# Feature-major up and gate products with stationary weight tiles in a fused two-block transformer kernel

## Chip, core and metric

One Trainium2 chip, one core. The metric is the device time of one execution in microseconds; inputs and weights lie in HBM, everything is float32.

## What is computed

Two transformer blocks one after the other on x of 256 tokens by 1024 features. The parts that the change touches are three feed-forward stages:

```python
# block 1, d_ff = 4096
h2 = rms_norm(x, g_mlp)
x = x + square(relu(h2 @ w_ff1)) @ w_ff2
x = x + sigmoid(rms_norm(x, g_ple) @ w_ple_gate) * (p @ w_ple)

# block 2, d_ff_2 = 2816, before and after its attention
x = x + 0.5 * ((silu(h @ w_gate) * (h @ w_up)) @ w_down)    # h = rms_norm(x, ffn_norm)
```

`rms_norm` divides a row by the root of its mean square and multiplies by a gain. Around these stand the projections and attentions of both blocks, which stay as they are.

## The kernel before

**Precision.** Every large product is done with three matmuls in float32r: an operand a is split into a_hi (a rounded to float32r by a copy) and a_lo = a - a_hi, and a_hi w_hi + a_hi w_lo + a_lo w_hi is summed in PSUM. Weights come in 163 units of 128x2048 (SyncE's queue, six raw slots). ScalarE makes w_hi (`hi`, L920), VectorE w_lo (`lo`, L1309). A unit is held until TensorE has counted it in `unit_used`; w_hi has four slots, w_lo lies in the raw slot. A narrow unit has four 128-row tiles of 512 columns, a wide one two of 1024.

**Layout.** Tokens lie on partitions in two row blocks tb of 128. Activations that are multiplied are first transposed: `turn` (L475, matmuls at L481) puts 128x128 blocks into a PSUM bank, `split` makes hi (ScalarE, L926) and lo (VectorE, L1316). `product` and `products` (L450, L458, matmuls at L467) take the transposed activation block (128x128) as the stationary operand and 512 columns of weights as the moving one; in the profile's names the moving operand stands first (`bank<-w_hi,hA_hi`).

**The three stages.** "ff" has 8 steps of 512 features, "f1" and "f2" 11 steps of 256 gate and 256 up features. A step i computes the up (and gate) products of step i into two banks `up(tb)` (`ff_up`, L665: two units, each over two row blocks), transposes the activations of step i - 1 in the middle (`ff_turn`, L659) and then multiplies those by the down weights into the four accumulator banks. The first step of a stage (`ff_up0`, L654) starts with row block 0 while the norm's operand of block 1 is still being made. ScalarE applies relu or silu with the row scale 1/rms out of the bank (L1076, L1149), VectorE multiplies with the bank's content (L1522, L1595) into act_f and frees the bank with `up_out`. In a gated stage's tail (L752 to L763) the last up products go by row block (`narrow_block`), with the transposes in between.

**Order.** Each engine's program is written out by hand; the engines meet only at semaphores. TensorE's order decides; the others run ahead as far as slots allow. GpSimd computes 1/rms (L1812, L1813, L1882) and loads gains.

Of the kernel before, what the change touches and what calls it, by code (L numbers as in the profile page):

```python
# [28 lines left out]
P = 128  # L29
D, TB, SEQ = 1024, 2, 256  # L30
# [63 lines left out]
def work_batches():  # L94
# [17 lines left out]
    order += [("ff", i, tb) for i in range(DFF // HALF) for tb in range(TB)]  # L112
    order += [("ple", tb, h) for tb in range(TB) for h in range(2)]
    order += [("ffn1", tb, h) for tb in range(TB) for h in range(2)]
    order += [("f1", i, tb) for i in range(FF2 // SUB) for tb in range(TB)]
# [9 lines left out]
    order += [("f2", i, tb) for i in range(FF2 // SUB) for tb in range(TB)]  # L125
# [3 lines left out]
def score_maps():  # L129
# [23 lines left out]
    [x for x in WB if x[0] in ("p", "ya", "yr", "m", "ff", "f1", "f2", "cq", "ckv", "cat", *NORMS)])}  # L153
# [6 lines left out]
def two_blocks(nc, x_d, p_d, g_mix, w_in, lam_q1, lam_k1, lam_q2, lam_k2, g_diff, g_ret, w_bd, w_br, w_out,  # L160
# [39 lines left out]
    hA = [sb(f"hA_{s}", [P, KT, SEQ], f32r) for s in ("hi", "lo")]  # L200
# [12 lines left out]
    def lay(start, *parts):  # L213
# [14 lines left out]
    qk_tm = lay(named["yr"], ("qk_tm0", [P, TB, HALF]), ("qk_tm1", [P, TB, HALF]))  # L228
    lam_v, lam_w = lay(named["ga"], ("lam_v", [P, 4, DHD]), ("lam_w", [P, 2, DHD]))
# [6 lines left out]
    fT0, fT1, act_r, act_f, pl_s, sg, pT0, pT1, p_sb, gain_mid = lay(  # L236
        arena, ("fT_hi", [P, 4, SEQ], f32r), ("fT_lo", [P, 4, SEQ], f32r), ("act_r", [P, TB, HALF]),
        ("act_f", [P, TB, HALF]), ("pl_s", [P, TB, D]), ("sg", [P, TB, D]),
        ("pT_hi", [P, 2, SEQ], f32r), ("pT_lo", [P, 2, SEQ], f32r), ("p_sb", [P, TB, 256]), ("gain_mid", [P, D]))
# [23 lines left out]
    up = lambda tb: bank[4 + tb]  # L263
    score = lambda name: bank[4 + SM[name] % 2]
    work = lambda name: bank[6 + WB[name] % 2]
# [10 lines left out]
    nhalf_ready, act_warm = sem("nhalf_ready"), sem("act_warm")  # L276
# [21 lines left out]
    up_done, act_ready, up_out = sem("up_done"), sem("act_ready"), sem("up_out")  # L298
# [124 lines left out]
    def rows_of(name):  # L423
# [6 lines left out]
        if kind in ("ff", "f1", "f2"):  # L430
            tb, k0, n, pair = name[2], 0 if kind == "ff" else 2 * (name[1] % 2), 4 if kind == "ff" else 2, fT
        elif kind == "cq":
            tb, k0, n, pair = name[1], 0, 3, cT
        else:
            tb, k0, n, pair = name[1], 4 * name[2], 4, hB if kind in ("ya", "m", "ple") else hA
# [13 lines left out]
    def _(pe):  # L449
# [204 lines left out]
        def ff_up0(u0, norm):  # L654

            narrow_block(up(0)[:, :], norm, u0, 0, HALF, lambda: src_turn(norm, 1)).then_inc(up_done, 1)
            narrow_block(up(1)[:, :], norm, u0, 1, HALF)

        def ff_turn(name, i, done, cols, di=0, blocks=range(TB)):  # L659

            for tb in blocks:
                pe.wait_ge(up_out, done - 1 + tb + 2 * di)
                turn((name, i, tb), [act_f[:, tb, j * P:(j + 1) * P] for j in range(cols // P)], di)

        def ff_up(u, name, i, steps, cols, du=0, di=0):  # L665

            for j in range(2):
                for tb in range(TB):
                    if j == 0:
                        pe.wait_ge(up_out, 2 * steps - 1 + tb + 2 * di)  # L670
                    mm = products([up(tb)[:, :]], hA, 4 * j, 4, tb, u + j, HALF, j == 0, j == 1, du)
                    if j and tb == 0:
                        mm.then_inc(up_done, 1)
                mm.then_inc(unit_used, 1)
                if j == 0:
                    ff_turn(name, i - 1, 2 * steps, cols, di)
# [3 lines left out]
        ff_up0(u, "mlp")  # L680
# [3 lines left out]
        def relu_step(i, r=0, start=False):  # L684
            v = U0["ff"] + 2 + 4 * (i - 1)
            ff_up(v, "ff", i, i, HALF, 12 * r, 3 * r)
            for j in range(2):
                for tb in range(TB):
                    if j == 0:
                        turned(("ff", i - 1, tb), 3 * r)  # L690
# [10 lines left out]
        ff_turn("ff", last, 2 * (last + 1), HALF)  # L701
# [1262 lines left out]
```

## Time and profile before

| | |
|---|---|
| runs | 1019.32 to 1019.88 us, median 1019.78 (3 runs) |
| the profiled execution | 1019.78 us, its span 1018.0 us |
| TensorE busy, of the span | 992.1 us (97%) in 4730 matmuls |
| VectorE busy | 578.5 us (57%) |
| ScalarE busy | 489.1 us (48%) |
| GpSimd busy | 72.3 us (7%) |
| DMA | 179.27 MB, mean 176 GB/s |

A matmul's record is longer than the distance to the next one, since matmuls are pipelined: distances between starts tell the price. PEld is the load of the stationary operand, which has a record of its own.

### The profile page before, as it was taken

The page shows a single profiled execution, that of the slowest core. Times are in us where ns is not written, and L with a number is a line of the kernel's source. Part 1 is how long each engine was busy: PE and PEld are TensorE (multiplying, and loading weights), DVE is VectorE, ACT ScalarE, POOL GpSimd, SP SyncE. Part 2 cuts the span into 40 slices and gives each one's busy share as a digit, 9 for nine tenths or more (in the row PEclk, how much of TensorE's full clock was granted, in tenths as well). Part 3 has the DMA queues.
Part 4 walks back from the last instruction along what each step waited for, and adds up shares of the span by engine and source line. Part 5 has one row for each costly group of instructions (what it writes and reads, how often), then busy time and mean ns, then how long its engine had stood idle before and what let it go on. Part 6 is the DMA issues. An engine that isn't in the chain of part 4 may idle for free.

```text
span 1018.0 us, 12693 instructions
## 1 busy us (share of the span) xinstructions
PE 992.1 (97%) x4730; PEld 821.4 (81%) x4730; DVE 578.5 (57%) x700; ACT 489.1 (48%) x613; POOL 72.3 (7%) x95
## 2 busy tenths in 40 slices
PE   6999999999999999999999999999999999999997
PEld 4888788888888888888778888888877888888885
DVE  4655555487675555555775455447555675555443
ACT  5545455744355344444563434335557454444431
POOL 3100000040020000000320000001111000000000
PEclk9999999999999999999999999999999999999999
DMA  9755545444465555454555555545552165556531
GB/s 322 249 193 167 163 134 187 144 154 186 165 238 207 192 186 185 171 200 166 203 174 202 177 195 183 188 149 176 175 204 65 44 208 184 196 177 205 168 122 42
DMA packets 99744, 179.27 MB, mean 176 GB/s; under 512 B 5856, under 2 KB 53872, under 8 KB 99696
## 3 DMA queue, kind: packets, MB, share of 16 engines
q1 hardware_dynamic: 97424, 171.99, 48.7%
q0 software_dynamic: 1984, 6.30, 2.0%
q8 instruction: 31, 0.51, 0.2%
q10 hardware_dynamic: 288, 0.33, 0.1%
q14 instruction: 17, 0.14, 0.0%
HBM read 177.55 MB, written 1.05 MB: 175 GB/s over the span
## 4 chain that ended last, share of the span: by engine, by line
PE 93%; DVE 3%; ACT 1%; issue 1%; POOL 1%; DMA 1%; DVEq 0%; POOLq 0%; ACTq 0%
PE bank L467 84%; PE bank L481 5%; PE bank L517 1%; PE bank L516 1%; DVE w_lo L1309 1%; DMA masks<-const_masks 1%; PE bank L528 0%; PE bank L530 0%; PE bank L529 0%; POOL rs L1813 0%; POOL ms L1812 0%; DVE x L1561 0%; PE bank L794 0%; PE bank L793 0%; DVE sg L1560 0%
## 5 line engine op out<-in xcount | busy, mean ns | idle before, releaser
L1309 DVE TENSOR_TENSOR w_lo<-raw,w_hi 128x2048 fp32r<-128x2048 f32 (+2 forms) x163 | 370.9, 2280 | 221.0 <-ACT w_hi L920 220.9
L920 ACT ACTIVATE w_hi<-raw 128x2048 fp32r<-128x2048 f32 (+2 forms) x163 | 308.1, 1891 | 159.9 <-PE bank L467 157.2
L467 PE MATMUL bank<-w_hi,hA_hi 128*128 128x512 f32 (+1 forms) x880 | 343.0, 396 | 5.1 <-DVE w_lo L1399 3.0
L467 PE MATMUL bank<-w_hi,hA_lo 128*128 128x512 f32 (+1 forms) x880 | 337.1, 389 | 0.0
L467 PE MATMUL bank<-w_lo,hA_hi 128*128 128x512 f32 (+1 forms) x880 | 336.7, 389 | 0.0
L467 PEld LDWEIGHTS bank<-w_hi,hA_hi 128*128 128x128 f32 x880 | 165.4, 188 | 38.7 <-issue 4.7
L467 PEld LDWEIGHTS bank<-w_hi,hA_lo 128*128 128x128 f32 x880 | 165.6, 188 | 34.7
L467 PEld LDWEIGHTS bank<-w_lo,hA_hi 128*128 128x128 f32 x880 | 165.9, 188 | 32.4
L467 PE MATMUL bank<-w_hi,fT_hi 128*128 128x512 f32 x304 | 93.8, 390 | 0.0
L467 PE MATMUL bank<-w_lo,fT_hi 128*128 128x512 f32 x304 | 93.6, 389 | 0.0
L467 PE MATMUL bank<-w_hi,fT_lo 128*128 128x512 f32 x304 | 93.6, 389 | 0.0
L926 ACT ACTIVATE fT_hi<-bank 128x256 fp32r<-128x256 f32 (+1 forms) x60 | 23.4, 439 | 117.4 <-PE bank L481 117.4
L467 PEld LDWEIGHTS bank<-w_lo,fT_hi 128*128 128x128 f32 x304 | 57.1, 188 | 11.9
L467 PEld LDWEIGHTS bank<-w_hi,fT_lo 128*128 128x128 f32 x304 | 57.1, 188 | 11.9
L467 PEld LDWEIGHTS bank<-w_hi,fT_hi 128*128 128x128 f32 x304 | 56.8, 188 | 11.6
L1316 DVE TENSOR_TENSOR fT_lo<-bank,fT_hi 128x256 fp32r<-128x256 f32 (+1 forms) x60 | 27.1, 491 | 62.6 <-ACT fT_hi L926 62.5
L1812 POOL TENSOR_SCALAR ms<-ss 128x1 f32<-128x1 f32 x16 | 7.8, 486 | 628.1 <-ACT junk L944 628.0
L1149 ACT ACTIVATE act_r<-bank,rs 128x256 f32<-128x256 f32 x44 | 20.9, 475 | 57.5 <-PE bank L467 55.0
L1595 DVE SCALAR_TENSOR_TENSOR act_f<-bank,rs,act_r 128x256 f32<-128x256 f32 x44 | 21.2, 481 | 21.6 <-ACT act_r L1149 21.6
L973 ACT ACTIVATE L<-L,mn 128x128 f32<-128x128 f32 x64 | 28.4, 458 | 10.1 <-DVE mn L1356 10.0
L944 ACT ACTIVATE junk<-x 128x1024 bf16<-128x1024 f32 x16 | 16.9, 1055 | 33.9 <-DVE x L1342 21.7
L467 PE MATMUL bank<-w_hi,hB_hi 128*128 128x512 f32 x96 | 30.2, 396 | 0.0
(236 smaller groups left out, 759.3 us busy)
## 6 DMA issues: line engine op xcount, KB each, us to landing
raw<-in_w_in SPq DMA_DIRECT2D x76, 512.0 KB, 4.5
raw<-in_w_ff SPq DMA_DIRECT2D x64, 512.0 KB, 3.9
raw<-in_ffn_w_gate SPq DMA_DIRECT2D x44, 512.0 KB, 3.6
raw<-in_ffn_w_up SPq DMA_DIRECT2D x44, 512.0 KB, 4.5
raw<-in_ffn_w_down SPq DMA_DIRECT2D x44, 512.0 KB, 4.0
raw<-in_w_out SPq DMA_DIRECT2D x16, 512.0 KB, 3.8
raw<-in_w_branch_diff SPq DMA_DIRECT2D x8, 512.0 KB, 3.7
raw<-in_w_branch_ret SPq DMA_DIRECT2D x8, 512.0 KB, 3.7
```

The costliest lines, as they stand in the source:

```text
L467: mm = pe.matmul(o, a, w, start=first and t == 0 and m < len(outs), stop=last and t == n - 1 and m >= len(todo) - len(outs))
L481: mm = pe.transpose(work(name)[0:cols, col:col + rows], blk, ident)
L516: pe.matmul(b[:, 0:P], q[:, h, 0:P], k[:, h, 0:P], start=True, stop=True)
L517: pe.matmul(b[:, P:384], q[:, h, P:SEQ], k[:, h, :], start=True, stop=True).then_inc(score_done, 1)
L920: act.activation(w_hi[u % HI_SLOTS][:, 0:w], raw[u % RAW_SLOTS][:, 0:w], ACT.Copy).then_inc(hi_ready, 1)
L926: act.activation(dst, b, ACT.Copy).then_inc(split_hi, 1)
L944: act.activation(junk[:, :], x[:, tb, :], ACT.Square, accum_out=ss[:, n:n + 1]).then_inc(square_sum, 1)
L973: e = act.activation(L[:, m % 4, c], L[:, m % 4, c], ACT.Exp, bias=mn[:, m, tb:tb + 1], scale=-1.0, accum_out=sm[:, m, tb:tb + 1])
L1149: act.activation(act_r[:, tb, 0:SUB], up(tb)[:, 0:SUB], ACT.Silu, scale=inv_rms(norm, tb))\
L1309: vec.tensor_tensor(w_lo[u % RAW_SLOTS][:, 0:w], raw[u % RAW_SLOTS][:, 0:w], w_hi[u % HI_SLOTS][:, 0:w].bitcast(f32), ALU.subtract).then_i ...
L1316: vec.tensor_tensor(dst, b, hi.bitcast(f32), ALU.subtract).then_inc(work_out[WB[name] % 2], 1)
L1595: vec.scalar_tensor_tensor(out=act_f[:, tb, 0:SUB], in0=up(tb)[:, SUB:2 * SUB], scalar=rs[:, n:n + 1], in1=act_r[:, tb, 0:SUB], op0=ALU.mu ...
```

## The change

The up and gate products change their operands' roles. For each 128-column weight tile f (four per step, `TILES`) and each k-tile there are two matmuls with the weight tile stationary: w_hi against h_hi and h_lo of all 256 tokens in one matmul of 512 columns (`both`; hA_hi and hA_lo now lie in one tensor hA2), and w_lo against h_hi, 256 columns (`one`). A bank `tall(f)` (banks 4 to 7) then holds 128 features by 256 tokens twice: the low half and a high half that belongs to h_lo. ScalarE copies one half out, VectorE adds the other (`tile_sum`), and the activation comes out with features on partitions, as the down products want it; `ff_turn` is gone. `f_split` makes hi and lo from SBUF.

A row scale is now a scale along columns. In "ff" it is left out of the activation and applied in `x_add` (relu(hr)^2 = r^2 relu(h)^2). In the gated stages the gate is multiplied by rsb, 1/rms spread over all partitions: GpSimd makes diagonal matrices (`rstd_rows`, `diag`), TensorE multiplies them by ones into bank 0 ahead of the last quarter of the first step, VectorE copies that out. The up half's scale goes with the 0.5 into `x_add` (`rsh`).

The first step (`first_tiles`) goes by row block and unit: 64 pairs of matmuls of 256 and 128 columns. The last step of a gated stage goes tile by tile like the others, with no work between. The transposes of "mlp", "ffn1" and "ffn2" go to the accumulator banks, as banks 6 and 7 are in use.

```diff
+        def tall_product(f, u, t, kt, cols, first, last):
+            at = t * HALF + f * P
+            hi, lo = w_hi[u % HI_SLOTS][:, at:at + P], w_lo[u % RAW_SLOTS][:, at:at + P]
+            both = halves(f)[:, :, cols], hi, hA2[:, :, kt, cols]
+            one = halves(f)[:, 0, cols], lo, hA2[:, 0, kt, cols]
+            for m, operands in enumerate((one, both) if last else (both, one)):
+                mm = pe.matmul(*operands, start=first and m == 0, stop=last and m == 1, skip_group_check=True)
+            return mm
+        def first_tiles(name, norm, order, beside=None):
...
+            for tb in range(TB):
+                cols = slice(tb * P, (tb + 1) * P)
+                for j in range(2):
+                    turned((norm, tb, j))
+                    if tb and j and beside:
+                        beside()
+                    pe.wait_ge(lo_ready, u + j + 1)
+                    for n, f in enumerate(order):
+                        for t in range(4):
+                            mm = tall_product(f, u + j, t, 4 * j + t, cols, (tb, j, t) == (0, 0, 0),
+                                              (tb, j, t) == (1, 1, 3))
...
+        def tiles(name, u, i, order, du=0, ds=0):
+            s = STEP0[name] + i
             for j in range(2):
-                for tb in range(TB):
+                pe.wait_ge(lo_ready, u + j + 1 + du)
+                for n, f in enumerate(order):
                     if j == 0:
-                        pe.wait_ge(up_out, 2 * steps - 1 + tb + 2 * di)
-                    mm = products([up(tb)[:, :]], hA, 4 * j, 4, tb, u + j, HALF, j == 0, j == 1, du)
-                    if j and tb == 0:
+                        pe.wait_ge(up_out, TILES * (s - 1) + n + 1 + TILES * ds)
+                    for t in range(4):
+                        mm = tall_product(f, u + j, t, 4 * j + t, slice(0, SEQ), (j, t) == (0, 0), (j, t) == (1, 3))
+                    if j and n < TILES - 1:
                         mm.then_inc(up_done, 1)
                 mm.then_inc(unit_used, 1)
-                if j == 0:
-                    ff_turn(name, i - 1, 2 * steps, cols, di)
...
+            def rstd_rows():
+                pe.wait_ge(ones_ready, 1)
+                pe.wait_ge(diag_ready, TB * (GATED[name] + 1))
+                for tb in range(TB):
+                    mm = pe.matmul(bank[0][:, tb * P:(tb + 1) * P], ones[:, :], diag[:, tb, :], start=True, stop=True)
+                mm.then_inc(rsb_done, 1)
+
+            first_tiles(name, norm, PAIRED, rstd_rows)
...
             v, i = u + 2 + 3 * (n - 2), n - 1
-            pe.wait_ge(up_out, 2 * (base + i))
-            narrow_block(up(0)[:, :], None, v, 0, HALF, lambda: ff_turn(name, i - 1, 2 * (base + i), SUB))\
-                .then_inc(up_done, 1)
-            narrow_block(up(1)[:, :], None, v, 1, HALF, lambda: ff_turn(name, i, 2 * (base + n), SUB, blocks=(0,)))
+            tiles(name, v, i, PAIRED)
             down(v + 2, i - 1, 0)
-            ff_turn(name, i, 2 * (base + n), SUB, blocks=(1,))
             down(v + 3, i, 0, last=True).then_inc(acc_done, 1)
...
+            # ScalarE, gated stages
+            def silu(i, k, r=0):
+                last_unit = u + 1 + (3 * i - 1 if i else 0)
+                for n, f in ((2 * k, k), (2 * k + 1, 2 + k)):
+                    half_copy(name, i, n, f, act_s[:, f, :], last_unit, 4 * r, 12 * r)
+                act.wait_ge(gate_in, PAIR0[name] + 2 * i + k + 1 + 8 * r)
+                act.activation(act_r[:, k, :], act_s[:, k, :], ACT.Silu).then_inc(gate_out, 1)
...
+            # VectorE, gated stages
+            def multiply(i, k, r=0):
+                tile_sum(name, i, 2 * k, k, act_s[:, k, :], 4 * r)
+                vec.tensor_tensor(act_s[:, k, :], act_s[:, k, :], rsb[:, :], ALU.mult).then_inc(gate_in, 1)
+                tile_sum(name, i, 2 * k + 1, 2 + k, act_s[:, 2 + k, :], 4 * r)
+                vec.wait_ge(gate_out, PAIR0[name] + 2 * i + k + 1 + 8 * r)
+                vec.tensor_tensor(act_f[:, k, :], act_r[:, k, :], act_s[:, 2 + k, :], ALU.mult).then_inc(act_ready, 1)
...
-                x_add(name, 0, 0.5, norm_out)
+                x_add(name, 0, half_rs[0], norm_out)
                 split_rows(norm_out, 0)
-                x_add(name, 1, 0.5, norm_out)
+                lo(v + 5)
+                x_add(name, 1, half_rs[1], norm_out)
```

## Rows read from the trace of the kernel before

**Rows 1.** The page: busy us, share and instructions of each engine; granted clock by slice.
```profile
PE 992.1 (97%) x4730; PEld 821.4 (81%) x4730; DVE 578.5 (57%) x700; ACT 489.1 (48%) x613; POOL 72.3 (7%) x95
...
PEclk9999999999999999999999999999999999999999
```

**Rows 2.** The page, chain that ended last: share of the span by engine.
```profile
PE 93%; DVE 3%; ACT 1%; issue 1%; POOL 1%; DMA 1%; DVEq 0%; POOLq 0%; ACTq 0%
```

**Rows 3.** Windows, a ReLU and a gated step: us, busy (instructions) of PE, PEld, DVE, ACT, POOL, clock.
```profile
379.16:401.84 22.68, 22.68 (x106) 18.88 (x105) 11.75 (x8) 9.91 (x8) 0.00 (x0) 1.00 0.51 185
526.90:543.70 16.80, 16.80 (x78) 13.90 (x77) 8.61 (x8) 7.12 (x8) 0.00 (x0) 1.00 0.56 189
```

**Rows 4.** The chain in order of time (start, us, what): the transposes of either kind of step.
```profile
401.82 0.87 PE bank L481 x8
...
543.28 0.44 PE bank L481 x4
```

**Rows 5.** Timeline of PE (start, us, shape) at 512 and 288 columns; the chain at 384.
```profile
400.06 0.39 PE L467 MATMUL bank<-w_hi,hA_lo 128*128 128x512 f32 x1
...
401.42 0.40 PE L467 MATMUL bank<-w_hi,hA_lo 128*128 128x512 f32 x1
...
708.13 0.29 PE L467 MATMUL bank<-w_hi,hA_hi 128*128 128x288 f32 x1
...
714.39 0.29 PE L467 MATMUL bank<-w_hi,hA_lo 128*128 128x288 f32 x1
...
751.97 3.15 PE bank L467 x18
```

**Rows 6.** Timeline of PE: float32 products of 64 columns, two instructions each.
```profile
766.03 0.39 PE L792 MATMUL bank<-mv,aT 128*128 128x64 f32 x2
766.25 0.39 PE L793 MATMUL bank<-mv,aT 128*128 128x64 f32 x2
```

**Rows 7.** The first gated stage's tail: two pieces of the chain, then PE's timeline.
```profile
675.42 5.48 PE bank L467 x24
681.12 5.47 PE bank L467 x24
...
693.11 0.66 PE L481 MATMUL bank<-masks,src 128*128 128x128 f32 x4 [0.39 <-DVE src L1335]
```

**Rows 8.** PE's timeline around the first gated stage's first two steps.
```profile
511.75 0.66 PE L481 MATMUL bank<-masks,src 128*128 128x128 f32 x4 [1.28 <-DVE src L1335]
512.16 0.47 PE L467 MATMUL bank<-w_hi,hA_hi 128*128 128x512 f32 x1
512.47 0.39 PE L467 MATMUL bank<-w_lo,hA_hi 128*128 128x512 f32 x1
...
522.94 0.39 PE L467 MATMUL bank<-w_hi,hA_lo 128*128 128x512 f32 x1
523.45 0.50 PE L467 MATMUL bank<-w_hi,hA_hi 128*128 128x512 f32 x1
```

**Rows 9.** GpSimd there, from the timeline; then a line's instructions, ns min/median/max.
```profile
517.48 2.47 POOL L1813 TENSOR_TENSOR rs<-ms,nhalf 128x1 f32<-128x1 f32 x1
520.03 2.27 POOL L1882 TENSOR_TENSOR rs<-rs 128x1 f32<-128x1 f32 x1
...
L1823 POOL TENSOR_SCALAR bias<-masks x8: 511/512/2652, 25.3 to 153.1; 128x384 f32<-128x384 f32 x8
```

**Rows 10.** Groups by line and form: busy us, mean ns of one, idle before.
```profile
L1309 DVE TENSOR_TENSOR w_lo<-raw,w_hi 128x2048 fp32r<-128x2048 f32 x157 | 362.2, 2311 | 219.1 <-ACT w_hi L920 219.0
...
L1595 DVE SCALAR_TENSOR_TENSOR act_f<-bank,rs,act_r 128x256 f32<-128x256 f32 x44 | 21.2, 481 | 21.6 <-ACT act_r L1149 21.6
...
L926 ACT ACTIVATE fT_hi<-bank 128x256 fp32r<-128x256 f32 x44 | 14.7, 382 | 86.5 <-PE bank L481 86.5
```

**Rows 11.** Timeline at the second gated stage's start: GpSimd's second scale, VectorE's w_lo.
```profile
828.44 0.56 POOL L1813 TENSOR_TENSOR rs<-ms,nhalf 128x1 f32<-128x1 f32 x1
...
829.88 4.48 DVE L1309 TENSOR_TENSOR w_lo<-raw,w_hi 128x2048 fp32r<-128x2048 f32 x2
```

## What the change does to the time, told before it was run

> **What bounds the kernel now.** I read the page from its totals downwards. TensorE is busy for 97% of the span, and the slices give it the full granted clock throughout, so no part of the sum rests on the clock [rows 1]. VectorE and ScalarE are near half [rows 1], so they matter only where someone waits for them. The chain that ended last is 93% TensorE: 84% of the span are the products of L467, 5% the transposes of L481 [rows 2]. A change here is worth what it takes from or adds to TensorE's instruction stream, plus waits at the joints of stages. The stages show no slack: a whole ReLU step lasts 22.68 us and a whole gated step 16.80 us, with TensorE busy in all of it and VectorE and ScalarE in about half [rows 3]. The chain in order of time splits such a step into 96 (72) products and 0.87 (0.44) us for 8 (4) transposes [rows 4].
>
> A busy time says little about a pipelined product: its record lasts 389 ns, but the next begins 0.227 us later. All prices below are distances between starts.
>
> **The price of a product by width.** 512 columns: from 400.06 to 401.42 are six distances, 0.227 us each [rows 5]. 384 columns: 3.15 us for 18, 0.175 [rows 5]. 288 columns: 708.13 to 714.39 is 47 distances, 0.133 [rows 5]. The line through 512 and 288 has 0.419 ns a column; 256 columns lie just beyond its end, at 0.120. There is also a floor that does not come from the columns: float32 products with only 64 columns, each with a stationary load of its own, still come 0.11 apart (two start at 766.03, the next two at 766.25) [rows 6]. So a product with 128 columns costs 0.110, not the 0.067 of the line.
>
> Here a rule bears on the case. The load floor of 0.11 is what the rows show [rows 6]. The Trainium skill (TensorE: Matmul & The Clock Gate, "LDWEIGHTS") gives a load as the stationary columns over 1.2, 107 ns for 128; by that rule, the trace agrees. The same page ("Packing small matmuls", on what overlaps) has loads overlap with products only where row groups differ, which speaks against a change that makes 16 more loads a step; by it 27 steps would take 27 x 16 x 0.107 = 46 us more (an estimate from that page). The 288-column products, 0.133 apart with a load each, leave no room for that [rows 5].
>
> **Removed: the transposes of the activations.** The ReLU stage has 8 steps with 8 each, 8 x 0.87 = 7.0 us. Each gated stage has ten steps' worth of 4 (0.44) and two pairs in its tail: 675.42 plus 5.48 is 680.90 and the next piece starts at 681.12, 0.22 a pair [rows 7]. That is 2 x (10 x 0.44 + 2 x 0.22) = 9.7. Together 152 transposes (64 and 88) and -16.6 us. The figure includes the slow first product behind each block (0.31 instead of 0.227, as from 512.16 to 512.47) [rows 8]. All of it is on the path.
>
> **Changed: the up and gate products.** Before, a step takes 8 k-tiles x 2 row blocks x 3 products of 512 columns: 48 x 0.227 = 10.90 us. After, 8 k-tiles x 4 weight tiles x (one of 512 and one of 256 columns): the columns are the same 24,576, the instructions are 64. Cost 32 x (0.227 + 0.120) = 11.10, so +0.21 a step. There are 8 + 11 + 11 = 30 steps, of which 27 are whole: +5.6 us. The bounds: with 256 columns at the load floor of 0.110 the step costs 10.78 and the 27 give -3.1; at the nearest measured fp32r width, 0.133, they give +16.8. I take 0.120, since three widths lie near one line and the nearest is only 32 columns away.
>
> **The first step of each stage** is cut by row block, since the second block's operand arrives later. It has 64 pairs of 256 and 128 columns: 64 x (0.120 + 0.110) = 14.7 against 10.90, +3.8 a stage, +11.5 for three. This is where the change pays most: the 128-column product does half the work of a 256-column one for nearly the same price. Bounds for it: 0.067, if the load hides entirely (-2.8 a stage), and 0.22, the two instructions of 0.11 that a float32 product takes [rows 6] (+7 a stage). No fp32r product under 288 columns is in the trace; I take 0.110 as the load floor is nearest to what binds.
>
> **The joints.** Before the first gated stage TensorE stands 1.28 us for src before the transposes of 511.75 [rows 8]; the first quarter's extra 0.9 us hides in it: -0.9. Then its three remaining quarters of 3.7 us begin at 512.16: two end at 519.5. There the new stationary-ones products wait for diag, which GpSimd makes behind the second rs. GpSimd's small operations stretch to VectorE's end of w_lo (2.47 us from 517.48; 2.27 from 520.03, just behind the start of the next w_lo) [rows 9]. In the new order VectorE waits for rsb after L1309's pair, so the second of these should take about 0.2, at 520.2. The two diag of 128 columns, a third of the 384 that take 0.51 [rows 9], take 0.3 each; with the hops diag is there at 521.0: +1.5. The ones products are 2 x 2 float32 instructions of 0.11 and a slow first one: 0.5 in each gated stage, +1.0. The wait of 0.28 before 523.45 goes (the new step's banks are four, freed in turn): -0.3 [rows 8]. In the second gated stage the second rs is there at 829.0 and TensorE comes to it eight microseconds later, so that diag is covered even if it waits until 834.4 for the w_lo of 829.88 [rows 11].
>
> At the end of a gated stage the last step's activations are no longer computed beside the second row block. After the last tile there are a ScalarE copy 0.38, a VectorE sum 0.48, a product 0.48, ScalarE's split 0.38 and VectorE's 0.48, with hops near 2.5 us [rows 10]; TensorE has 12 products (2.73 us) before it asks. Just covered: 0, and up to +1 in each if a hop is longer. Moving w_lo of the next unit behind the first x_add takes away the 0.39 wait at 693.11 [rows 7]: -0.4, though it delays the second x_add by some 0.6.
>
> **What hides the vector work.** A gated step gets four ScalarE copies, four VectorE sums, two products by rsb and the same two products of gate and up; the conversions L920 and L1309 stay, and x_add does the same operation with its scale read from a tile. VectorE: 3 x 2.29 + 10 x 0.45 = 11.4 of 16.6 us; in a ReLU step 4 x 2.29 + 12 x 0.45 = 14.6 of 22 [rows 10]. The deadline is the bank: tile n of the next step needs up_out n. The first tile is ready 9.6 us before TensorE returns to it, and so is each next one. Queued in front of its sum stands one w_lo, which starts 7.5 us into the step and ends at 9.8; the four sums are out by 13.0 and the first is wanted at 16.6. Cost nothing; were this cover gone, every late microsecond would count 27 times.
>
> **Sum.** -16.6 + 5.6 + 11.5 - 0.9 + 1.5 + 1.0 - 0.3 - 0.4 = +1.4 us on a span of 1018.0. The profiled execution took 1019.78, 1.8 more than its span, and is the median itself: 1021.2. The transposes saved are given back in halves: to the fixed part of more, shorter products and to the three cut first steps.
>
> **Rivals.**
> *The short product is cheaper.* If the 256-column product runs at the load floor, every step wins: 27 x 32 x 0.010 = 8.6, and 3 x 64 x 0.010 = 1.9 in the first steps: 1010.7. For it: eight transposes with a load each take 0.87, the slow product behind them included, so not over 0.109 each [rows 4]. Against it: three fp32r widths all carry about 13 ns [rows 5]. The Trainium skill (TensorE: Matmul & The Clock Gate, "Back-to-back issue gap") has columns/2.4 + 2.5 ns for a single product, 109 ns for 256; it also makes 512 cost 216, where the trace has 227. Chance 0.15, 1008 to 1015.
> *The short product is dearer*, the rival on the slower side. One mechanism: fp32r widths under the measured ones do not follow the line, since the load becomes what is waited for. At 0.133 for both short widths: 27 x 32 x 0.013 + 3 x 64 x (0.013 + 0.023) = 18, 1039; with only the 128-column ones at 0.22, 3 x 64 x 0.11 = 21, 1042. It decides from 0.121 upwards for the 256-column product, so a nanosecond counts 1 us. For it: nothing that narrow was run, and loads and columns nearly tie (0.110 and 0.107). Against: the floor and the line both lie under 0.121. Chance 0.25, 1028 to 1042.
> *Waits replace transposes.* The hand-over between three engines in tails and joints, or ScalarE's hand-back of gate_in and gate_out, comes late, by 5 to 14 us in all: 1026 to 1035. Against it is the slack of 3.6 us in every step. Chance 0.1.
>
> **How the numbers follow.** Forecast 0.5, 1018 to 1025. About 0.2%, 2 us, is what a measurement can tell from no change: faster means under 1017.7, slower over 1021.8. The forecast lies close to that upper line and gives 0.05, 0.25 and 0.2 to faster, same and slower; the others 0.15 faster and 0.35 slower. Faster 0.2, same 0.25, slower 0.55. The range 1010 to 1034 holds the forecast, nearly all of the cheap case, the waits and the nearer end of the dear one: 0.8.
>
> **What would show it.** In the new profile: no transposes of act_f; distances of 0.227 and 0.120 in turn in a whole step, which should last 22.0 (ReLU) and 16.6 us (gated); 14.7 us for a first step's 128 products; TensorE standing about 1.5 us ahead of the first ones products; no TensorE wait for VectorE sums inside steps. A distance of 0.110 or 0.133 makes the prediction wrong by itself.

## The result and the profile after

| | before | after |
|---|---|---|
| median of the runs | 1019.83 us (1019.32 to 1020.01) | 1029.3 us (1027.99 to 1031.62) |
| the profiled execution, its span | 1019.78, 1018.0 us | 1028.2, 1026.4 us |
| ratio, 95% interval | | 1.0096 (1.008 to 1.0112) |
| predicted | | 1021.2 (1010 to 1034) |

The changed kernel is slower by about 9.5 us, 1%. The forecast gave 0.55 to slower, and slower it is, but by more: its likeliest case, 1018 to 1025, did not come. The time lies inside the range, 8 us above the point, where two of the rivals had put theirs ("the short product is dearer", 1028 to 1042, and "waits replace transposes", 1026 to 1035). That the range held is in part luck, since neither rival's mechanism accounts for most of it.

The page of the changed kernel, busy time by engine and then the chain's shares:

```profile
PE 998.8 (97%) x5258; PEld 847.4 (83%) x5258; DVE 641.3 (62%) x898; ACT 516.3 (50%) x733; POOL 71.7 (7%) x104
...
PE 93%; DVE 3%; ACT 1%; issue 1%; POOL 1%; DMA 1%; DVEq 0%; POOLq 0%; ACTq 0%
```

Against [rows 1] and [rows 2] the shape is the same: TensorE is 97% busy and 93% of the chain, now with 528 more matmuls. By line, the pages give the chain of before 84% of products (L467) and 5% of transposes (L481), and that of the changed kernel 53% (L482) and 33% (L676, the changed ones) of products and 3% of transposes (L496). VectorE got 63 us of work and ScalarE 27, and neither became the bound. So the lost time has to be looked for in TensorE's own stream and at the joints.

The windows of a ReLU step, a gated step and, further down, two stretches behind the second block's attention (us, then busy and instructions of PE, PEld, DVE, ACT, POOL, then the granted clock):

```profile
332.68:354.83 22.15, 22.15 (x113) 18.82 (x113) 13.55 (x16) 10.08 (x12) 0.00 (x0) 1.00 0.55 190
...
543.25:559.97 16.72, 16.72 (x90) 14.32 (x89) 10.67 (x14) 8.28 (x11) 0.00 (x0) 1.00 0.57 188
...
812.00:816.00 4.00, 3.41 (x22) 3.13 (x22) 1.07 (x3) 0.50 (x2) 0.00 (x0) 0.82 0.01 4
816.00:818.00 2.00, 2.00 (x8) 1.63 (x7) 1.55 (x3) 0.85 (x2) 0.00 (x0) 0.51 0.00 0
```

A whole step did become shorter than before, 22.15 against 22.68 and 16.72 against 16.80 [rows 3], but not as short as forecast (22.0 and 16.6). In the last two stretches the granted clock is 0.82 and 0.51: it falls to its lower level of 1.2 GHz, half of the full one, which the forecast had nowhere.

Where the 8.4 us of span came in is read by putting the same places of the two chains side by side. First the chain of before (start, us, what): the last transposes ahead of "ff", the end of "ff", a copy behind "f1", two groups of transposes of the second block, the end of "f2".

```profile
289.79 0.87 PE bank L481 x8
...
494.37 0.56 issue
...
736.98 0.70 DVE mqT L1729
...
810.58 1.09 PE bank L481 x8
...
821.24 0.88 PE bank L481 x8
...
1010.65 1.30 DVE x L1640 x2
```

The same places in the chain of the changed kernel:

```profile
290.81 0.87 PE bank L496 x8
...
494.68 0.56 issue
...
740.94 0.70 DVE mqT L1803
...
814.51 1.97 PE bank L496 x8
...
826.76 0.87 PE bank L496 x8
...
1018.98 1.42 DVE x L1714 x2
```

The lag is 1.02, 0.31, 3.96, 3.93, 5.52 and 8.33 us. Its steps, with what the forecast's own terms give for each stage:

| stretch | forecast | measured |
|---|---|---|
| up to "ff" (first load of constants and what follows) | 0 | +1.0 |
| "ff": 3.8 + 7 x 0.21 - 7.0 | -1.7 | -0.7 |
| "f1": 4.6 for the joint and first step, + 10 x 0.21 - 4.8 - 0.4 | +1.5 | +3.65 |
| second block's attention up to 810.58 | 0 | 0.0 |
| 810.58 to 821.24, where the clock fell | 0 | +1.6 |
| "f2": 4.3 + 10 x 0.21 - 4.8 | +1.6 | +2.8 |
| sum | +1.4 | +8.35 |

### The profile page after: what moved, and what is told of

The parts are those of the page before. It is cut to its first block, busy times and chain, and to the rows that moved or that the text cites. A ratio compares the mean times of both kernels' runs of the same rounds, so it can differ in the third digit from the quotient of the medians.

```text
span 1026.4 us, 14193 instructions
## 1 busy us (share of the span) xinstructions
PE 998.8 (97%) x5258; PEld 847.4 (83%) x5258; DVE 641.3 (62%) x898; ACT 516.3 (50%) x733; POOL 71.7 (7%) x104
## 4 chain that ended last, share of the span: by engine, by line
PE 93%; DVE 3%; ACT 1%; issue 1%; POOL 1%; DMA 1%; DVEq 0%; POOLq 0%; ACTq 0%
PE bank L482 53%; PE bank L676 33%; PE bank L496 3%; PE bank L532 1%; PE bank L531 1%; DVE w_lo L1363 1%; DMA masks<-const_masks 1%; PE bank L543 0%; ACT junk L989 0%; DVE hA L1370 0%; PE bank L545 0%; PE bank L544 0%; POOL rs L1887 0%; DVE x L1396 0%; DVE sg L1629 0%
## 5 line engine op out<-in xcount | busy, mean ns | idle before, releaser
L676 PE MATMUL bank<-hA,w_hi 128*128 128x512 f32 (+1 forms) x1056 | 345.8, 385 | 1.3 <-issue 1.3
L676 PE MATMUL bank<-hA,w_lo 128*128 128x256 f32 (+1 forms) x1056 | 266.2, 271 | 0.0
L482 PE MATMUL bank<-w_hi,hA 128*128 128x512 f32 (+1 forms) x800 | 247.8, 392 | 4.1 <-DVE w_lo L1453 3.0
L676 PEld LDWEIGHTS bank<-hA,w_hi 128*128 128x128 f32 x1056 | 192.2, 188 | 32.4 <-issue 1.7
L676 PEld LDWEIGHTS bank<-hA,w_lo 128*128 128x128 f32 x1056 | 198.8, 189 | 9.5
L482 PEld LDWEIGHTS bank<-w_hi,hA 128*128 128x128 f32 x800 | 150.3, 189 | 34.8 <-issue 4.6
L482 PE MATMUL bank<-w_lo,hA 128*128 128x512 f32 (+1 forms) x400 | 150.2, 388 | 0.0
L482 PE MATMUL bank<-w_hi,fT_hi 128*128 128x512 f32 x304 | 93.9, 390 | 0.0
L482 PE MATMUL bank<-w_lo,fT_hi 128*128 128x512 f32 x304 | 93.6, 389 | 0.0
L482 PE MATMUL bank<-w_hi,fT_lo 128*128 128x512 f32 x304 | 93.6, 389 | 0.0
L482 PEld LDWEIGHTS bank<-w_lo,hA 128*128 128x128 f32 x400 | 75.9, 190 | 14.7
L1125 ACT ACTIVATE act_s<-bank 128x256 f32<-128x256 f32 x120 | 42.9, 375 | 69.1 <-PE bank L676 69.1
L482 PEld LDWEIGHTS bank<-w_lo,fT_hi 128*128 128x128 f32 x304 | 57.1, 188 | 12.0
L482 PEld LDWEIGHTS bank<-w_hi,fT_lo 128*128 128x128 f32 x304 | 57.1, 188 | 11.9
L482 PEld LDWEIGHTS bank<-w_hi,fT_hi 128*128 128x128 f32 x304 | 57.0, 188 | 11.0
L1577 DVE TENSOR_TENSOR act_s<-bank,act_s 128x256 f32<-128x256 f32 x120 | 50.2, 419 | 23.9 <-ACT act_s L1125 23.8
```

What stands on the lines that cost most here:

```text
L482: mm = pe.matmul(o, a, w, start=first and t == 0 and m < len(outs), stop=last and t == n - 1 and m >= len(todo) - len(outs))
L676: mm = pe.matmul(*operands, start=first and m == 0, stop=last and m == 1, skip_group_check=True)
L1125: act.activation(dst, halves(f)[:, 1, :], ACT.Copy).then_inc(half_out, 1)
L1577: vec.tensor_tensor(dst, halves(f)[:, 0, :], dst, ALU.add).then_inc(up_out, 1)
```

## Experiments

The first theory was that the excess in whole steps is a property of the product pair, 0.352 us where the sum has 0.347, that the first steps cost what was forecast, and that what is above 1028 in a run is the clock. The experiments change first the pair, then the first step, then the joint, and last the widths. The runs of before beside them had medians of 1019.85 (the first four kernels), 1020.33 (after_again to e8_all512) and 1019.98 us.

**The moving operand in one piece.** The `both` product reads h_hi and h_lo from two places 2048 elements apart. Here they lie side by side for each k-tile.

```diff
-            hA2 = sb("hA", [P, 2, KT, SEQ], f32r)
+            hA2 = sb("hA", [P, KT, 2, SEQ], f32r)
...
```

> The changed kernel with one thing different: h_hi and h_lo lie side by side per k-tile, so the 512-column product of a whole step reads one contiguous stretch instead of two of 256. In the changed kernel a pair costs 0.352 us, 0.234 from the 512-column product to the 256-column one and 0.118 back. Theory A, the two-stretch operand costs 7 ns: the 0.234 falls to 0.227, a whole step from 11.27 to 11.05, and the 27 steps give 5 to 6 us. Theory B, the 7 ns come from the order (a 512-column product whose stationary operand is loaded behind a short one): the distances stay, the time stays within 1 us of the changed kernel's at the same granted clock.

Measured: 1029.96 us (1028.35 to 1033.41), ratio to before 1.0089 (1.0069 to 1.0109), no different from the changed kernel. The up products of one step in its chain:

```profile
332.57 11.27 PE bank L683 x64
```

11.27 us again: how the operand lies plays no part. The profiled execution was the longest of these, 1033.41 us, with a mean clock of 0.991, and shows where this one lost its time. Its windows (columns as above):

```profile
508.00:510.00 2.00, 0.81 (x4) 0.84 (x5) 2.00 (x4) 2.00 (x4) 1.27 (x3) 0.67 0.93 314
510.00:514.00 4.00, 4.00 (x21) 4.00 (x20) 3.69 (x6) 2.26 (x2) 0.00 (x0) 0.50 0.28 100
...
524.00:526.00 2.00, 0.24 (x3) 0.12 (x2) 0.00 (x0) 1.75 (x1) 1.92 (x6) 0.94 0.27 26
526.00:532.00 6.00, 6.00 (x28) 6.00 (x29) 1.70 (x4) 1.91 (x4) 0.79 (x3) 0.50 0.70 254
```

Twice TensorE stood for longer, 2.90 us until 509.19 and 1.76 us until 525.98, and each time the clock was at 0.50 in the stretch behind it. Six microseconds at half the clock are three microseconds of work lost. Both stands belong to the first gated stage's start; the second is the wait for diag that the change added.

**All w_hi products of a tile, then all w_lo products.** Same products, another order.

```diff
-                    for t in range(4):
-                        mm = tall_product(f, u + j, t, 4 * j + t, slice(0, SEQ), (j, t) == (0, 0), (j, t) == (1, 3))
+                    for m in ((1, 0) if j else (0, 1)):        # 0: both, 1: one
+                        for t in range(4):
+                            mm = pe.matmul(*tall_operands(f, u + j, t, 4 * j + t, slice(0, SEQ))[m], ...)
...
```

> The changed kernel with another order inside a tile: four 512-column products (w_hi) one after the other, then four of 256 columns (w_lo), instead of alternating; operands as before. Theory B (a 512-column product behind a 256-column one starts late): only one in four still stands behind a short one, three in four fall to 0.227, a whole step from 11.27 to about 11.1, 4 us in all. Theory A (two-stretch operand): 512-column products stay at 0.234 wherever they stand, no gain. For the 256-column products in a row both say 0.118 to 0.120; at 0.133 the load would be what binds.

Measured: 1028.34 us (1026.95 to 1031.83), ratio 1.0073 (1.0057 to 1.009). A step in the chain:

```profile
332.51 11.20 PE bank L717 x64
```

and on TensorE's timeline (start, us, what):

```profile
400.02 1.09 PE L717 MATMUL bank<-hA,w_hi 128*128 128x512 f32 x4
400.95 0.63 PE L717 MATMUL bank<-hA,w_lo 128*128 128x256 f32 x4
401.42 1.09 PE L717 MATMUL bank<-hA,w_hi 128*128 128x512 f32 x4
```

11.20 instead of 11.27: the order gives back 0.07 a step, 1.9 us in 27, less than half of what was expected (the fastest run is 1.0 us under the changed kernel's fastest). Eight products take 1.40 us, 0.350 a pair. Part of the excess belongs to the change of width from one product to the next; the rest stayed.

**A cheaper first step.** The w_hi products stay cut by row block; the w_lo products are done once, for both row blocks, when the second one's operand is there: 96 products instead of 128.

```diff
-                        for t in range(4):
-                            mm = tall_product(f, u + j, t, 4 * j + t, cols, ...)
+                        if tb:
+                            for t in range(4):
+                                pe.matmul(*tall_operands(f, u + j, t, 4 * j + t, slice(0, SEQ))[1], ...)
+                        for t in range(4):
+                            mm = pe.matmul(*tall_operands(f, u + j, t, 4 * j + t, cols)[0], ...)
...
```

> The changed kernel with the first step of each stage done differently: w_hi products by row block as before (256 columns), but w_lo once for both row blocks (256 columns instead of twice 128), so 96 products instead of 128. Theory, the load sets the price of every short product: 96 x 0.120 = 11.5 instead of 14.7 us, 3.2 us less in the first and third stage. In the second most of it is lost, since TensorE then only waits longer for the diagonal matrices (1.8 us in the changed kernel, up to 4.5 here): 6.5 to 7.5 us in all. Rival, the columns set the price (128 columns cost half of 256): the columns are the same and nothing is gained.

Measured: 1024.22 us (1021.56 to 1024.91), ratio 1.0036 (1.0027 to 1.0046). The fastest execution (mean clock 0.998) is 6.4 us under the changed kernel's fastest, where 6.5 to 7.5 was expected; the others, at 0.994 to 0.997, are up to 3.4 us longer. The timeline shows the price of 256 columns among themselves:

```profile
298.81 0.64 PE L701 MATMUL bank<-hA,w_hi 128*128 128x256 f32 x4
299.29 0.64 PE L698 MATMUL bank<-hA,w_lo 128*128 128x256 f32 x4
```

From 298.81 to 299.29 are four products, 0.120 each: the value the line gave. The 0.120 was right for products of this width alone.

**The removed transposes, priced by doubling them.** The kernel before, with the transposes of the activations done twice.

```diff
-                turn((name, i, tb), [act_f[:, tb, j * P:(j + 1) * P] for j in range(cols // P)], di)
+                turn((name, i, tb), [act_f[:, tb, j * P:(j + 1) * P] for j in range(cols // P)], di, 2)
...
```

> The kernel before with each transpose of the activations done twice into the same bank: 152 more. If they cost on the path what the prediction's sum takes for their removal, 8 take 0.87 and the added ones have no slow product of their own: 152 x 0.109 = 16.6 less some 20 x 0.08 and 8 x 0.08 for that product, so 14 to 16.6 us more than before. Rival, they partly fill gaps in which TensorE would wait for the activations anyway: under 10 us more, and a wait of TensorE would shrink in the trace.

Measured: 1037.27 us (1036.76 to 1038.73), ratio 1.017 (1.0153 to 1.0187), +17.4 us. A group in its chain:

```profile
382.25 1.75 PE bank L482 x16
```

Twice 0.87 [rows 4]: the second eight cost what the first eight do. The 17.4 lies a little over the 14 to 16.6 that was expected, and well over the rival's limit of 10: no wait was hidden behind the transposes. What this prices is adding them. That removing them gave the same is seen in a whole step: 22.15 us are 11.27 of up products and 10.88 of down products, with nothing between. So the miss lies in what was added.

**The changed kernel again**, beside the next ones.

> The changed kernel itself, for the spread of its times against the granted clock. In the two kernels derived from it the granted clock fell to 0.50 behind TensorE's stands of 1.5 to 2.5 us at the first gated stage's start (506 to 510 and 524 to 526) and cost some 2.5 us each time; the profiled execution of the changed kernel had none there and took 1028.2. Theory: its executions fall into levels, about 1028 without such a fall and 2 to 3 us higher for each, with a lower mean clock; the kernel before has the first of the two stands too, but seldom a fall. Rival: the spread has nothing to do with the clock, times and clock are not ordered alike.

Measured: 1028.87 us (1028.05 to 1031.30), ratio 1.0092 (1.0077 to 1.0108); mean clock 0.997 in the shortest, 0.995 in the longest. Time and clock are ordered alike, but the levels that were expected (1028 without a fall of the clock, 2 to 3 us more for each) are not there: in the profiled execution, 1028.40 us, the clock was at 0.50 from 510 to 512 and at 0.72 to 514, behind a stand of 2.55 us.

**The scale's rows behind the first step.** The ones products follow the whole first step instead of standing ahead of its last quarter; VectorE's and ScalarE's copies and sums of step 0 go ahead of rsb.

```diff
-            first_tiles(name, norm, PAIRED, rstd_rows)
+            first_tiles(name, norm, PAIRED)
+            rstd_rows()
...
```

> The changed kernel with the products by ones put behind the first step instead of ahead of its last quarter, and the first step's copies and sums ahead of the multiplication by rsb on ScalarE and VectorE. TensorE then reaches diag after it is there: the stand of 1.8 us goes, up to 1 us of it may come back as a wait for rsb or for the first sums at step 1: 1 to 2 us less than the changed kernel in an undisturbed execution. If the stand also brings the clock down, the median gains 1 to 2 us more. Rival: something else is late then by as much, and the first whole step starts at the same time.

Measured: 1026.56 us (1025.1 to 1028.76), ratio 1.0065 (1.0051 to 1.0079): 3.0 us less in the fastest run and 2.3 in the median. The chain at the first gated stage's start:

```profile
506.02 2.54 issue
508.56 5.44 PE bank L676 x32
...
514.89 11.09 PE bank L676 x96
525.98 0.44 PE bank L775 x4
526.42 11.18 PE bank L676 x64
```

The stand ahead of the ones products is gone. What that is worth shows best beside the trace of after_again, which has the same stand ahead of the stage (2.55 us) and the same fall of the clock behind it: there the down products of step 1 start at 539.57, here at 537.61, 1.96 us earlier, and the whole execution is 1.84 us shorter. That is the stand (1.76 there) and little else; what the fastest runs have beyond it, 1.1 us, isn't explained.

Another stand remains, 2.54 us ahead of the stage's first product, which the chain puts down to "issue". The traces settle what it is. The product waits for the low part of hA, as in the kernel before (0.90 us until 507.01, put down to `hA_lo`): VectorE writes it in two operations, 1.28 us together, from 507.77 here and from 506.88 in the changed kernel, and the stage's first product starts behind the first of them, at 508.56 and 507.67. VectorE is late by one earlier operation, the product `sg`, which ran beside GpSimd's product of two gains. First this run, then the changed kernel:

```profile
495.00 2.38 POOL L1968 TENSOR_TENSOR gain<-gain,gain_mid 128x1024 f32<-128x1024 f32 x1 [4.76 <-DMA gain<-in_ffn_norm]
495.58 2.35 DVE L1633 TENSOR_TENSOR sg<-sg,pl_s 128x512 f32<-128x512 f32 x1 [5.13 <-ACT sg L1172]
...
494.11 2.39 POOL L1959 TENSOR_TENSOR gain<-gain,gain_mid 128x1024 f32<-128x1024 f32 x1 [3.50 <-DMA gain<-in_ffn_norm]
495.96 1.08 DVE L1629 TENSOR_TENSOR sg<-sg,pl_s 128x512 f32<-128x512 f32 x1 [5.13 <-ACT sg L1171]
```

The next `sg`, with GpSimd idle, takes 0.69. In all twelve traces of this document the stand is 0.1 to 0.2 us longer than this `sg`: 0.90 to 1.28 where it took 0.78 to 1.08 (before, e4_turn_twice, the changed kernel, e3_first, e6_best), and 2.22 to 2.90 where it took 2.03 to 2.71 (the other seven). How far the two operations overlap hangs on when the load of the gain lands, and that differs between two executions of the same kernel: GpSimd waited 3.50 us for it in the changed kernel's first trace and 4.78 in after_again's.

**All of it together.** The order of e2_grouped, the first step of e3_first, and the ones products behind the second weight tile of step 1, with VectorE's and ScalarE's splits of step 0 ahead of the next unit's conversion.

```diff
                 for n, f in enumerate(order):
+                    if beside and (j, n) == (0, 2):
+                        beside()
...
+            for m, f in enumerate((0, 2, 1, 3)):
+                tile_sum(name, 0, m, f, act_s[:, f, :])
+            lo(u + 4)
...
-                lo(v + 3, 12 * r)
+                if i > 1:
+                    lo(v + 3, 12 * r)
                 for k in range(2):
                     f_split(name, i - 1, k, 2 * ((i - 1) % 2) + k, 8 * r)
+                if i == 1:
+                    lo(v + 3, 12 * r)
...
```

> The parts together: w_lo once per stage start (96 instead of 128 products), four long and four short products in a row in whole steps, and the products by ones only after the second weight tile of step 1, with the activations of step 0 reordered on ScalarE and VectorE. From 1028.0 undisturbed: 27 x 0.07 = 1.9 for the order, 3.2 each in the first and third stage, 3.2 in the second as the wait for diag no longer stands in the way, and 1.5 of the stand: 1028.0 - 13.0 = 1015, some 0.4% under the kernel before. Rival: the second stage's start is held by the chain from rms through GpSimd whatever the order, so that its 4.7 us stay: 1019.5, no difference to the kernel before.

Measured: **1016.79 us** (1016.49 to 1018.04), ratio 0.9968 (0.9956 to 0.998), faster than both kernels, by 0.3% than the one before. 1015 was expected. The chain:

```profile
519.35 2.80 PE bank L724 x16
...
522.59 8.41 PE bank L724 x48
```

and the window of the joint (columns as above):

```profile
506.00:520.00 14.00, 12.11 (x97) 11.54 (x96) 11.24 (x14) 9.14 (x14) 6.46 (x10) 1.00 0.37 120
```

TensorE still stands for 1.9 of these 14 us, in two pieces of 0.50 and 1.40, behind one of 1.25 just before, and the clock stays whole. e3_first had nearly the same three (1.03, 0.50, 1.40), and there it fell behind them, to 0.50 from 510 to 512; so it isn't shown that the shape of the stands is what kept it. The three savings in the fastest runs come near: 1028.05 - 1.9 (e2) - 6.4 (e3) - 3.0 (e5) = 1016.7 beside 1016.49, partly by luck, since the 3.0 is 1.1 more than the traces explain. The runs lie closer together than the changed kernel's, 1.6 us instead of 3.3; those of before beside them span 1.7.

**Every product 512 columns.** The w_lo product multiplies h_lo too (this adds the term of the two low parts to the result): new roles of the operands at the old width.

```diff
-            one = halves(f)[:, 0, cols], lo, hA2[:, 0, kt, cols]
+            one = halves(f)[:, :, cols], lo, hA2[:, :, kt, cols]
```

> The changed kernel with w_lo against both halves of h, so that the products of whole steps all have 512 columns (it adds the low-low term; the first steps' w_lo products have 256). 512-column products cost 0.234 in the changed kernel, 0.230 in a row of four, 0.227 in the kernel before. Theory, mixing widths costs: among equals they come 0.227 apart, 64 x 0.227 = 14.5 us a step. Rival, the new roles cost (weights stationary, h moving): 0.230 to 0.234, 14.7 to 15.0 us a step. The time is 27 x 3.3 to 3.7 higher, near 1120.

Measured: 1117.57 us. A step's 64 products:

```profile
336.32 14.51 PE bank L676 x64
```

0.2267 each, what 512 columns cost in the old roles [rows 5]. A stationary weight tile instead of a stationary activation block costs nothing in itself.

**The second product 288 and 384 columns wide**, in the layout of e1_contiguous (either adds a part of the low-low term). L says that a load has to fit behind the product before it, M that a change of width costs something by itself.

```diff
-            return both, (halves(f)[:, 0, cols], lo, hA2[:, kt, 0, cols])
+            if cols == slice(0, SEQ):
+                return both, (tall(f)[:, 0:288], lo, hA2[:, kt].rearrange("p s t -> p (s t)")[:, 0:288])
+            return both, (halves(f)[:, 0, cols], lo, hA2[:, kt, 0, cols])
```

> The contiguous form of the changed kernel, with the w_lo product of whole steps widened from 256 to 288 columns (32 columns of the low-low term are added). At equal widths the new roles cost 0.2267 us for 512 columns, and 256-column products in a row 0.120, so that a pair should cost 0.347; it costs 0.352 alternating and 0.350 in fours. Theory L, the next load hardly fits behind 256 columns (two loads in a first step's pair take 0.230, 0.115 each, against 0.120): with 288 columns it fits, and the pair costs what the line says, 0.227 + 0.133 = 0.360, 11.52 us a step. Theory M, unequal widths in turn cost 5 ns whatever they are: 0.365, 11.68 us a step.

> As the run with 288 columns, with 384. Theory L: 0.227 + 0.175 = 0.402, 12.85 to 12.9 us a step. Theory M: 0.407, 13.0 us a step.

Measured: 1038.42 and 1082.53 us. The up products of a step at 288:

```profile
332.86 11.62 PE bank L685 x64
```

and at 384:

```profile
335.22 13.07 PE bank L685 x64
```

Together with the others, against the sum of the two widths' own prices (0.227, 0.175, 0.133, 0.120):

| second product | pair | sum of its parts | excess |
|---|---|---|---|
| 256, in turn | 0.352 | 0.347 | 5 ns |
| 256, in fours | 0.350 | 0.347 | 3 ns |
| 288, in turn | 0.363 | 0.360 | 3 ns |
| 384, in turn | 0.408 | 0.402 | 6 ns |
| 512 | 0.453 | 0.453 | 0 |

At 384 columns a load of 0.11 fits easily and the excess is the largest, so L has fallen. What holds is M's bare statement: pairs of unequal width cost 3 to 6 ns more than their parts, pairs of equal width nothing. What makes it so was not found: M expected the same excess at every width, and it isn't quite. Two things go together in all these pairs and were not separated, the width of the moving operand and the part of the bank that is written. The two widened forms and the one with 512 columns were run once each; their rows are of steps at full clock.

## Why the prediction was off, step by step

**The whole steps' products: the term that was mis-sized.** The forecast took 0.227 + 0.120 for a pair, 11.10 a step and +5.6 us in all. TensorE's timeline of the changed kernel:

```profile
400.03 0.40 PE L676 MATMUL bank<-hA,w_hi 128*128 128x512 f32 x1
400.26 0.28 PE L676 MATMUL bank<-hA,w_lo 128*128 128x256 f32 x1
400.38 0.40 PE L676 MATMUL bank<-hA,w_hi 128*128 128x512 f32 x1
...
401.79 0.40 PE L676 MATMUL bank<-hA,w_hi 128*128 128x512 f32 x1
```

From 400.03 to 401.79 are five pairs, 0.352 each; a step's 32 take 11.27. The 27 whole steps so cost 27 x 0.37 = +10.0 instead of +5.6: 4.4 us of the miss of 7. Both single prices were right (e3_first: 0.120; e8_all512: 0.227), only their sum was not the pair's. The prediction said that a nanosecond on this product counts 1 us, and gave the forecast's own range, 1018 to 1025, room for under four of them: five came. No row of before has a pair of unequal widths; the working did not name this gap.

The Trainium skill (TensorE: Matmul & The Clock Gate, "Back-to-back issue gap") gives a single product as columns over 2.4 and 2.5 ns more, 109 ns for 256. The runs show 120, so the rival that leaned towards it had the wrong sign. The same page's rule that a load overlaps only with products of other row groups (in its part "Packing small matmuls") does not hold here either: 256 columns with a load each, all rows used, came 0.120 apart.

**The first steps: right.** The chain of the changed kernel (start, us, what), "ff" and then "f1":

```profile
294.45 3.65 PE bank L676 x32
...
298.98 11.09 PE bank L676 x96
...
522.17 0.68 PE bank L775 x4
522.85 14.96 PE bank L676 x96
```

3.65 + 11.09 = 14.74 for the 128 products of "ff"; 14.7 was forecast. A pair of 256 and 128 columns takes 0.230, the 0.120 + 0.110 of the forecast. Only the pair is measured: no run has 128-column float32r products among themselves, so that the 0.110 holds alone is not shown. This was the place where the change paid most, and e3_first got more than half of it back by doing 32 products fewer in each stage.

**The transposes: right.** -16.6 was forecast, e4_turn_twice has 17.4 (15.6 to 19.1 by its interval), and the chain has none in the steps.

**The first gated stage's joint: right in kind, 0.9 too small.** Forecast +4.6 up to the start of step 1, measured +5.5. GpSimd and TensorE there, from the timeline:

```profile
518.10 2.47 POOL L1887 TENSOR_TENSOR rs<-ms,nhalf 128x1 f32<-128x1 f32 x1
...
520.65 0.19 POOL L1967 TENSOR_TENSOR rs<-rs 128x1 f32<-128x1 f32 x1
...
520.82 1.20 POOL L1903 TENSOR_SCALAR diag<-masks,rs 128x128 f32<-128x128 f32 x2
...
522.17 0.68 PE L775 MATMUL bank<-diag,ones 128*128 128x128 f32 x4 [1.80 <-POOL diag L1903]
```

The mechanism is the one told: the first rs stretched to 2.47, the second done in 0.19 while VectorE waits, then the diagonals, and TensorE standing. But each diagonal takes 0.60, not 0.3: I had scaled 0.51 for 384 columns [rows 9] by the columns, and that row multiplies by a constant where this one reads a scale for every partition (that this makes the difference is not shown). The 0.9 is made of three parts: the stand was 1.80 instead of 1.5, the ones products took 0.68 instead of 0.5, and the stage's first product came 0.35 late, as the stand ahead of it grew from 0.90 to 1.28 with VectorE's `sg` (under e5_late_rows). In the second gated stage there is no such stand, as forecast; its ones products cost 0.50 and the stage's start +4.3.

**The tails: right.** No wait where I had allowed 0 to +1; ahead of the stage's last piece the 0.39 of [rows 7] has gone.

**What hides the vector work: right.** In no step does TensorE wait for a sum or a copy.

**The clock: left out.** I read the whole clock on the page of before [rows 1] and let no part of the sum rest on it. That was true of the trace of before, but the page can't show it: its slices are 25 us long, and the page of the changed kernel has the same row of nines. In that kernel's profiled execution the clock fell once, between 814 and 818 us (windows above). The eight transposes that took 1.09 in before, with the clock at 1.00 and the same stand of 0.59 ahead of them, took 1.97, and the stretch to 826.76 lost 1.6 us. No edit of this change is at that place, and in e2_grouped it fell there too, so this 1.6 is a matter of the execution.

At the first gated stage's start it fell in most traces of the changed forms. Directly behind the stand ahead of the stage it fell to about 0.50 in each of the seven traces where that stand was 2.22 to 2.90 us, and not in before, e4_turn_twice, the changed kernel and e6_best (0.90 to 1.28; e3_first fell only behind its next two stands). Behind the wait for diag, 1.76 to 1.91 us in seven traces, it fell in four (e1_contiguous, e2_grouped, e3_first, e10_one384) and not in the changed kernel, after_again and e9_one288, nor in e8_all512, where the wait was 1.46. So the forecast priced a stand of TensorE at its own length, and in some executions it cost more: in e1_contiguous the stretch behind the second stand lost three more microseconds.

The changed kernel's runs, ordered, are 1027.99 (mean clock 0.999), 1028.2 (0.997), 1030.4 (0.995) and 1031.62 (0.993). That the clock makes the whole spread is argued, not shown: the mean holds the kernel's last microseconds at 0.50 too, and e6_best has 0.997 without any other fall. Taking 1.6 and 1.8 us for the falls off the two profiled executions, 1028.2 and 1028.40, leaves 1026.6 for both, an estimate, and none of the eight executions was that short. Before spans 0.7 us in the four executions of the result and 2.8 in the thirteen beside the first experiments.

**The first microseconds.** +1.0 us up to "ff" is the load of the constants (5.90 us after, 5.26 before) and 0.35 in the projection ahead of "ff", where the edit does nothing. Neither is of the change's terms. But the first part is not noise of the changed kernel: the load took 5.87 to 6.13 us in all ten traces of the changed forms, 5.76 in e4_turn_twice and 5.26 in the one trace of before. Why was not tried.

Sum of the miss on the span, 8.4 - 1.4 = 7.0: pairs 4.4, joint 0.9, clock 1.6, start 1.0, which is 7.9; the 0.9 too much is 0.1 in "ff" and 0.4 in each gated stage, where nothing was found for it. The median lies another 1.1 us above the profiled execution. Of the rivals, "dearer" came nearest: its mechanism (a load that isn't hidden) was wrong, but its warning that one nanosecond decides was right. "Waits replace transposes" held in one joint only.

**Open.** Why products of unequal width cost 3 to 6 ns more in turn. Whether the clock falls behind a stand of 1.8 us: it did in some traces and not in others. And what the changed kernel gains if GpSimd's product of the gains is moved away from VectorE's `sg`: it was not tried.

## What to carry to other kernels

Price a stream of products as the stream that it will be: the price of each width by itself was right to the nanosecond here, and the pair was 5 ns dearer, which 864 pairs made 4.4 us. When a wide product is cut for the sake of an early start, count the narrow products at the 0.11 us or so that even 128 columns cost, and do them once for all pieces. A stand of TensorE at a joint can cost more than its length, when the clock falls behind it: move small waiting products behind work that is ready, rather than ahead of it (1.8 to 2.0 us here between two traces with the same clock). And where a wait is put down to "issue", follow the engine that makes the operand back through its own operations: here one on VectorE had stretched from 0.8 to 2.4 us beside one of GpSimd, and TensorE stood as much longer.

## What the runs showed of the hardware

- float32r products one after the other: 0.227 us at 512 columns, 0.175 at 384, 0.133 at 288, 0.120 at 256; with 128 columns in turn with 256, 0.230 a pair.
- Unequal widths in turn: 3 to 6 ns a pair above that; equal widths: none.
- A moving operand in two pieces 2048 elements apart cost the same as one in a single piece.
- Directly behind stands of TensorE of 2.22 to 2.90 us the granted clock fell to about 0.50 in seven traces of seven; behind stands of 1.76 to 1.91 us in four of seven. In e1_contiguous it stayed there for 4 and 6 us.
- Stands of 1.25, 0.50 and 1.40 us close together left it at 1.00 (e6_best); 1.03, 0.50 and 1.40 did not (e3_first).
- VectorE's 128x512 product of two tensors took 0.69 us with GpSimd idle and 2.03 to 2.71 where GpSimd's 128x1024 product ran beside it for most of that time.
- GpSimd: 0.60 us for a 128x128 multiplication with a scale per partition, against 0.51 for 128x384 with constants [rows 9].
